# Products of constants in TensorE's pauses, and two more panel steps behind the first head's scores

## What is computed

```python
def first_block(x, mem, ...):            # per layer
    h = x @ w_in[l]                      # 1024 -> 7328
    o_mla  = softmax attention, 8 heads (low-rank q and kv, rope)
    o_diff = 8 heads, softmax(q1 k1) - lambda * softmax(q2 k2), rms per head
    o_mem  = 4 heads of attention on mem
    merged = g0*(o_mla @ wb0) + g1*(o_diff @ wb1) + g2*(o_mem @ wb2)
    x = layernorm(alpha*x + merged @ w_out)
    x = layernorm(alpha*x + relu(x @ w1)**2 @ w2)

def second_block(x, p, ...):             # per layer
    u = rmsnorm(h)
    y_ssd, y_hg, y_ml = three bidirectional scans on slices of u @ w_in
    h = h + (sum of gate_i * (y_i @ w_br_i)) @ w_out
    h = h + gated convolved MLP(rmsnorm(h));  h = h + (p @ w_ple) * sigmoid(h @ w_ple_gate)
```

## Time and profile before

| | |
|---|---|
| time, three runs | 2723.05, 2731.67, 2734.22 us; median 2731.67 |
| the profiled execution | 2721.62 us, its span 2719.8 us |
| TensorE busy | 2516.7 us (93%) |
| VectorE, ScalarE, GpSimd busy | 1808.8 (67%), 1434.1 (53%), 215.1 us (8%) |
| mean granted clock of TensorE | 0.968 |
| chain that ended last, by engine | PE 67%, DVE 19%, ACT 8%, issue 4% |
| read from HBM | 422 MB, 156 GB/s over the span |

### The profile page before, as it was taken

One profiled execution on the slowest core, in us unless ns is written; L12 is line 12 of the kernel. 1 busy time (PEld: TensorE's weight loads), 2 busy tenths in 40 slices (PEclk: granted clock), 3 DMA queues, 4 the chain that ended last, 5 costly groups with the idle time before them and its releaser, 6 DMA issues.

```text
span 2719.8 us, 42209 instructions
## 1 busy us (share of the span) xinstructions
PE 2516.7 (93%) x17296; PEld 2305.4 (85%) x17296; DVE 1808.8 (67%) x2918; ACT 1434.1 (53%) x2099; POOL 215.1 (8%) x191
## 2 busy tenths in 40 slices
PE   8998999999989999879899979999979899979998
PEld 7887989988779898778898778997878897778997
DVE  4566676565566755667678776875567678776875
ACT  4645545445464544546565534654545555535654
POOL 0000000000000000000017300000000117300000
PEclk9999999989999999889999989999989999989999
DMA  7553456555435566534377535665623467535664
GB/s 228 161 142 93 141 177 193 190 157 156 125 86 171 174 202 206 140 93 114 101 199 198 161 101 176 190 198 178 167 71 109 127 190 194 156 109 172 194 198 132
DMA packets 358958, 426.24 MB, mean 157 GB/s; under 512 B 21208, under 2 KB 286894, under 8 KB 358766
## 3 DMA queue, kind: packets, MB, share of 16 engines
q1 hardware_dynamic: 342890, 401.95, 49.1%
q10 hardware_dynamic: 14068, 15.91, 2.7%
q0 software_dynamic: 1808, 5.69, 0.6%
HBM read 422.35 MB, written 1.15 MB: 156 GB/s over the span
## 4 chain that ended last, share of the span: by engine, by line
PE 67%; DVE 19%; ACT 8%; issue 4%; DMA 1%; ACTq 0%; POOL 0%; DVEq 0%
PE ps L112 65%; DVE wlo L121 4%; ACT whi L118 3%; PE ps L115 2%; DVE sE L121 2%; ACT hgKm L118 1%; DVE hgA L148 1%; ACT E L118 1%; DVE hgQF L121 1%; ACT L118 1%; DVE hgQB L121 1%; DVE sz L130 1%; DVE E L124 1%; DVE hgkf L121 1%; DVE ys L130 1%
## 5 line engine op out<-in xcount | busy, mean ns | idle before, releaser
L121 DVE TENSOR_TENSOR wlo<-wring,whi 128x1024 fp32r<-128x1024 f32 x768 | 927.2, 1219 | 567.0 <-ACT whi L118 566.6
L118 ACT ACTIVATE whi<-wring 128x1024 fp32r<-128x1024 f32 x768 | 801.0, 1053 | 431.2 <-PE ps L112 419.2
L112 PE MATMUL ps<-uT,whi 128*128 128x256 f32 x4896 | 879.3, 284 | 30.8 <-DVE uT L121 28.1
L112 PEld LDWEIGHTS ps<-uT,whi 128*128 128x128 f32 x4896 | 761.3, 193 | 38.9 <-issue 37.8
L112 PE MATMUL ps<-uT,wlo 128*128 128x256 f32 (+1 forms) x2448 | 689.6, 282 | 0.0
L112 PEld LDWEIGHTS ps<-uT,wlo 128*128 128x128 f32 (+1 forms) x2448 | 470.2, 192 | 0.0
L112 PE MATMUL ps<-xT,whi 128*128 128x256 f32 x2112 | 386.7, 287 | 3.9 <-DVE xT L121 3.5
L112 PEld LDWEIGHTS ps<-xT,whi 128*128 128x128 f32 x2112 | 328.1, 191 | 11.0 <-issue 7.5
L112 PE MATMUL ps<-xT,wlo 128*128 128x256 f32 x1056 | 298.8, 283 | 0.0
L112 PE MATMUL ps<-whi,hid 128*128 128x512 f32 x864 | 267.9, 389 | 0.0
L112 PEld LDWEIGHTS ps<-xT,wlo 128*128 128x128 f32 x1056 | 202.7, 192 | 0.3
(11 more groups left out here) (373 smaller groups left out, 3516.8 us busy)
## 6 DMA issues: line engine op xcount, KB each, us to landing
wring<-in_w_in SPq DMA_DIRECT2D x346, 512.0 KB, 4.0
wring<-in_mlp_w SPq DMA_DIRECT2D x128, 512.0 KB, 4.5
wring<-in_w_up SPq DMA_DIRECT2D x88, 512.0 KB, 4.4
wring<-in_w_down SPq DMA_DIRECT2D x44, 512.0 KB, 4.2
wring<-in_w_branch SPq DMA_DIRECT2D x32, 512.0 KB, 3.6
wring<-in_w_out SPq DMA_DIRECT2D x32, 512.0 KB, 3.8
wring<-in_mem_w_kv SPq DMA_DIRECT2D x16, 512.0 KB, 5.3
mxb<-spread ACTq DMA_DIRECT2D x32, 256.0 KB, 5.6
```

Of the source, the lines that this page charges most:

```text
L112: return self.e.matmul(*p, **k) if self.e else Nothing()
L118: return self.e.activation(*p, **k) if self.e else Nothing()
L121: return self.e.tensor_tensor(*p, **k) if self.e else Nothing()
```

## The change

A new step `busy(u, n)` waits until the bank u is free and the identity has landed, and issues n products of the identity with 256 columns of constants into u. Nobody reads them; the bank's next step overwrites them. Such steps are put in: 4 products ahead of each LayerNorm's turn; 16 (layer 0) and 7 (layer 1) ahead of the mix norm's turn; 4 ahead of the turn of the small gates; 9 ahead of the products of level −1 of the first half in `hg_scan`; 4 and 17 ahead of the first panel of branches 0 and 1. The ffn norm's turn gets none. In all 103 products.

`staged` gets `first`: that many yields ahead of i = 1, so that more steps of the other generator lie between the first head's scores and everything that follows. It is 2 in `mla()`, `diff()` and `mem()`.

```diff
-def staged(n, *stages):
+def staged(n, *stages, first=0):
 
     for i in range(n + max(lag for _, lag, _ in stages)):
+        if i == 1:
+            for _ in range(first):
+                yield
         for f, lag, rest in stages:
...
             u = ring.take()
+            if wait and b0 == 0:
+                do("busy", u, wait)
...
         u = AB.take()
+        if wait:
+            do("busy", u, wait)
         do("narrow_turn", rows, u, nb)
...
-    def turned_by_halves(src, ready, out):
+    def turned_by_halves(src, ready, out, wait=0):
 
         us = [AB.take() for _ in range(4)]
+        if wait:
+            do("busy", us[0], wait)
...
-        turned_by_halves(n.res.tok(), lambda c, t: [("ln", n.tag, t, c // 4)], out)
+        turned_by_halves(n.res.tok(), lambda c, t: [("ln", n.tag, t, c // 4)], out, 4)
...
             yield from staged(8, (scores, 0, True), (lambda h: turn_unit(un[h]), 1, True),
-                              (lambda h: do("weights", un[h]), 0, False), (values, 2, True))
+                              (lambda h: do("weights", un[h]), 0, False), (values, 2, True), first=2)
...
             yield from staged(8, (scores(0), 0, True), (scores(1), 0, True), (lambda h: turn_unit(un[h, 0]), 1, True), (values, 2, True),
-                              (norm, 3, False), (weights, 0, False), (gain, 4, False))
+                              (norm, 3, False), (weights, 0, False), (gain, 4, False), first=2)
...
-        rms_turn(norm, l, "norm_mix_g_2", uT)
+        rms_turn(norm, l, "norm_mix_g_2", uT, 7 if l else 16)
...
-            yield from narrow([w[0:1024, SDT:SDT + 32], w[0:1024, LI:LI + 32]], uT, tb, "small_out", c)
+            yield from narrow([w[0:1024, SDT:SDT + 32], w[0:1024, LI:LI + 32]], uT, tb, "small_out", c, wait=4)
...
             do("hg_start", B)
-            do("hg_products", B, -1, [AB.take(), AB.take()])
+            us = [AB.take(), AB.take()]
+            if not hf:
+                do("busy", us[0], 9)
+            do("hg_products", B, -1, us)
...
-                yield from branch(acc, a[key][l], 0, x, gT[n], n, keep=True)
+                yield from branch(acc, a[key][l], 0, x, gT[n], n, keep=True, wait=(4, 17)[n])
...
+    def busy(u, n):
+
+        bank_free(u)
+        e.wait_ge(*at("ident"))
+        for _ in range(n):
+            e.matmul(u.ap[:, 0:256], ident, cst[:, 0:256], start=True, stop=True)
```

More of the change, by code:

```diff
@@ L445, in projA, with projB @@
                 yield
-    def projB(w, c0, n, x, out, r0=0, ring=PB):
+    def projB(w, c0, n, x, out, r0=0, ring=PB, wait=0):
         chunks = x.n // 512
@@ L461, in projB, with narrow @@
             yield
-    def narrow(parts, x, rows, kind, *args):
+    def narrow(parts, x, rows, kind, *args, wait=0):
         nb = 32 * len(parts)
@@ L800, in block1, with branch @@
         return xN2, xT2, lambda: ln_rows(n, gb, xN2)
-    def branch(acc, wb, r0, x, g, i, merged=None, keep=None):
+    def branch(acc, wb, r0, x, g, i, merged=None, keep=None, wait=0):
         for k in range(4):
@@ L812, in out @@
                     ar.give(acc.b[k])
-            yield from projB(wb, k * 256, 256, x, out, r0)
+            yield from projB(wb, k * 256, 256, x, out, r0, wait=0 if k else wait)
         if keep is None:
@@ L840, in after, with rms_turn @@
                 hkey[0], hkey[1] = ([(tag, i, 0), (tag, i, 1)] for i in range(2))
-    def rms_turn(n, l, g, x):
+    def rms_turn(n, l, g, x, wait=0):
         do("rms_scale", n)
-        turned_by_halves(n.u3, lambda c, t: [("rms", n.tag, t, c // 4)], to_pair_scaled(x, g, l))
+        turned_by_halves(n.u3, lambda c, t: [("rms", n.tag, t, c // 4)], to_pair_scaled(x, g, l), wait)
         ar.give(*n.hold)
@@ L1498, in ffn_columns @@
             e.transpose(us[i].ap[:, 0:88], pr.ap[0:88, i * 128:i * 128 + 128], ident[0:88, 0:88]).then_inc(*up("pe_turn", us[i].full))
-    parts = dict(tokens=tokens, features=features, turn=turn, turn_half=turn_half, narrow_turn=narrow_turn, columns=columns, rope_tables=rope_tables,
+    parts = dict(tokens=tokens, busy=busy, features=features, turn=turn, turn_half=turn_half, narrow_turn=narrow_turn, columns=columns, rope_tables=rope_tables,
                  latent_norm=latent_norm, scores=scores, turn_weights=turn_weights, mla_values=mla_values, values=values, diff_norm=diff_norm,
```

## The result

The changed kernel takes 2736.78 us (median of 20 runs, 2727.89 to 2751.55), the kernel before, on the same chip, 2728.45 (20 runs, 2717.96 to 2739.95): ratio 1.0033, 95% interval 1.0017 to 1.0048, so 5 to 13 us slower. The prediction was 2712, range 2700 to 2727, with 0.05 for slower by over 0.5%. The profiled execution has a span of 2735.7 us (before 2719.8) at a mean granted clock of 0.971 (0.968).

A forecast was written before the change was run, and what follows sets the result against it. TensorE, busy 93% of the span, was taken as the bound, losing time only in pauses and at half clock. −22.8 + 6.6 − 9.4 + 6.0 = −19.6 us, from 2731.67 to 2712, range 2700 to 2727.

The forecast's parts named there:

- 8.5 a layer, and 2.9 of clock: In `diff()`, two more steps remove 8.5 us of pauses and 2.9 us of half clock per layer; 22.8 us for both.
- the parting of the pairs: In `diff()`, panels now fall between the two scores of a head; the prediction said so and gave it no price.
- over 8 us of pauses: In `diff()`, the prediction calls itself wrong if over 8 us of pauses stay; it expected E waits of about 4 a layer.
- The products' clock, −9.4: At LayerNorms, mix norms and branches, products in the pauses save 9.4 us of half clock behind them; bounds 0 and 18.7.
- The 4.5 at the mix norms: Ahead of the mix norms' turns, products bring back 4.5 of 6.5 us, the clock falling late, over the turns.
- LayerNorms and branches were given 4.9: Ahead of LayerNorms' turns and branches, products bring back 0.4 of 12.2 us, 4.9.
- the question: At the filled pauses: whether a remaining pause of 2.1 to 3.3 us still brings TensorE's clock down.
- `hg_scan`, +6.0: In `hg_scan`, 9 products start its first level 2.98 us later, uncovered; +6.0 us for both layers, bounds +2 and +6.9.
- `mla()`, +6.6: At the end of `mla()`, a new pause of 2.2 us a layer plus 1.1 of half clock; +6.6 us for both layers.
- `mem()` at 0: In `mem()`, no pause and 3 to 5 panels between scores and turn either way, so 0 us.
- The third: Rival: the `diff()` pauses only move to another head's turn, `diff()` gives 0, +3.2 us, 2735; chance 0.08.

## Why the prediction was wrong

- **What fails is the step "8.5 a layer, and 2.9 of clock" in `diff()`, −22.8 in all.** The steps alone give +7 us there. A layer was to gain 11.4 us and loses 1.5 to 1.7, an error of 13. Three things make it up. First, the pauses shrank by 2.9 us, not 8.5: the panel count between scores and turn is not the only limit. A turn with two panels between still waits 2.27, and when a head's scores come late, the bank in the ring of four that they need is held by exponentials (2.75 us at 269.30). Second, the half clock stays at 10.2 us instead of giving 2.9, because two of the new pauses bring it again. Third, the parting of the pairs was seen and put at nothing without a reason: four more parted pairs a layer at 1.0 to 1.1 us, 4.2 of the 5.4 in the window. The trace before showed the price, a group x8 at the same 1.14 us as x4 at 1.13, and I had not read it. So the first two are 8.5 of the error and the pairs 4.2; it is the pairs that turn a small gain into a loss. The check that I named ("over 8 us of pauses") came out so, 10.0.
- **The products' clock, −9.4**: the term is mis-sized, it measures −0.5 (interval −4 to +2). The 4.5 at the mix norms is not shown: layer 1 gains 3.0 in the trace, and what layer 0 gains also comes without products. LayerNorms and branches were given 4.9. The fall came at 30 of the 45 places with 2.17 to 3.18 us left, so the question was the right one; why nothing is left in the time stays open.
- **`hg_scan`, +6.0**: right in mechanism, +5.0 by the offsets, and one for one at three times the size; not seen in the times of the 9 products.
- **`mla()`, +6.6**: right in mechanism, too high by more than half. The profile has +1.3 a layer, 2.6 in all; the new pause is 1.17 us instead of 2.2, and no half clock follows it. The timed run of these steps alone gives +1 (−3 to +5). `mem()` at 0 shows +0.2 a layer.
- **The sum of the parts**: +7 (diff), +1 (the other steps), −0.5 (94 products), +5 (the 9, by the profile), 12.5, to be set beside the 8 measured (5 to 13).
- **The rivals.** The third, with the diff pauses only moved, gave 2735, and 2736.78 was measured; it named the right place, and pauses did move in part, but `diff()` costs 7 us instead of 0. That its time comes so close is luck: it starts from the median of three runs, 2731.67, where 20 runs have 2728.45. As a difference it says +3.2, and +8.3 was measured. I had given it 0.08. The rivals all varied how much of a pause goes; none asked what else the new order changes for TensorE's own work.
- **Resolution.** Kernels that are the same in a stretch differ in it by up to 7 us in the offsets (1167 to 1910), since half clock and pace fall differently. Offsets that repeat in both layers and in several kernels, and that kernels without the change don't show, I take as real; differences over a whole run I do not.

## What to carry over

When an interleaving changes, look not only at how many panels lie between a step and its consumer but at what had been next to what: here two products on disjoint rows took the time of one only as neighbours, and a generator that yields between them gives that away. Filling pauses with idle products paid here when less than 1 us was left of them; with 2.2 to 3.2 us left the time stayed the same, and on a chain that is not covered by other work 27 products cost their full time. Idle time that a view of waits shows gone is not yet time won: compare the start of the same instruction in both traces, and in a third kernel that is the same there, to see how much such a difference is worth.

## What the runs showed of the hardware

- Two float32 matmuls of 64 rows each, on the lower and the upper half of the partitions, run at once when they are adjacent: 1.14 us for both scores, 1.13 for one, starts 13 ns apart.
- The half clock can come after the pause, over full-speed work: 1.4 us behind the end of 2.18 us (394.58 to 395.95), 1.6 at another LayerNorm (582.11 to 583.69). It does so behind 3.91 us too: 0.1 us behind its end in the kernel before (390.49 to 390.55), 1.4 in the run of the steps in `diff()` only. How long it lasts at one place differs between traces: 3.41, 6.83 or 10.24 us at the LayerNorms.
- A product of 128 x 256 float32 constants, back to back, takes 0.44 us (27 in 11.82); the matmul behind it starts 0.16 us before the modelled end.
- At granted clock 1.00 the same matmuls start 113 or 118 ns apart for 100 us and more (179 and 172 in 20 us).
